# Token-tile square sums issued two units later on TensorE, in the four phases that add to the residual x of a two-layer streaming encoder

## The chip, the cores and the metric

The kernel runs on one core of a Trainium2 chip. The core has five engines with an instruction stream each: TensorE (PE in the rows; its weight loads are PEld), VectorE (DVE), ScalarE (ACT), GpSimd (POOL) and SyncE (SP). The streams meet only at semaphores. Each engine takes its own instructions in order, so an instruction that waits holds up all behind it on that engine. The metric is the device time of one execution in microseconds; the kernel before takes 2903.98 us, the median of three runs (2901.82 to 2904.86).

## The reference

One step over 1024 prompt tokens and 32 sample tokens (1056 in all, 1024 features), two layers, all in float32:

```
for layer in (0, 1):
    x = x + mixer(rmsnorm(x))            # layer 0: RG-LRU + windowed attention, layer 1: mLSTM
    x = x + swiglu(rmsnorm(x))
    x = x + sigmoid(x @ w_gate) * (p[layer] @ w_proj)
y = rmsnorm(x)

rmsnorm(x) = x * rsqrt(mean(x*x over the 1024 features) + 1e-6) * g
```

What matters here is rmsnorm: for every token it needs the sum of squares over all features, so it can't begin for a token before all features of that token's x are done.

## The kernel before, in words

x lies in SBUF with the features on partitions: eight blocks of 128 features (`KT` = 8), each 1056 tokens wide. The tokens are cut into `NT` = 3 tiles of `TW` = 352 columns. Weights come in blocks of 128 output features. SyncE loads a block into one of two `raw` buffers (L400); GpSimd splits it into a high part `wh` (L427) and a low part `wl` (L429), 128x1024 each, in one of four slots, and may take a slot when TensorE has counted it free (`block_done`). A product of float32 precision is three matmuls, high by high, high by low, low by high (`hilo`, L385 to L387). A **unit** is the product of one weight block with one token tile: 8 times 3 = 24 matmuls of 352 columns into one PSUM bank of six.

Four phases add to x: `out0` and `out1` (the output projections of the two mixers) and `gate0` and `gate1` (the last line of each layer). Each is a `tail_phase` of 24 units, numbered 0 to 23 in the order of the table `TAIL` (`out0` starts at unit 8, since its first eight are made earlier). Units 12 to 15 are the last four feature blocks of token tile 0, units 16 to 19 those of tile 1, units 20 to 23 those of tile 2. So after unit 15 token tile 0 is complete, after 19 tile 1, after 23 tile 2. Units 20 to 23 are also the last use of a weight block each; each of them sets a slot free, and GpSimd then splits a block of the next phase into it. TensorE may write unit u when VectorE has emptied the bank of unit u - 6.

For a finished unit the engines do this:

- In the `out` phases VectorE adds the bank to x (L965). In the `gate` phases ScalarE makes the sigmoid of the bank (L1517), VectorE multiplies it with the projection (`prod`, L1033) and adds that to x (L1035).
- ScalarE squares the new x (L1432) into one of two buffers, and VectorE adds the squares into `sqsum` or `sqsum_o` (L895).
- When the squares of all eight feature blocks of a token tile are added, one float32 matmul with a matrix of ones sums them over the partitions (`norm_sum`, L456; the trace has two records for it). It waits for VectorE's add of the tile's last squares: **sum 0** for those of unit 15, **sum 1** for unit 19, **sum 2** for unit 23.
- ScalarE takes the root (`rt`, L1398), VectorE the reciprocal (`rstd`, L857). Then for each of the eight feature blocks VectorE scales x (`tmp`, L906; in `gate1`, where the final norm is made, `ybuf`, L901), ScalarE copies the result to `xh` (L1403), and VectorE subtracts to get `xl` (L914).

VectorE's order around the sums is fixed (`tail_phase` in the vector block). After the add of unit 17 and the squares of 16: reciprocal and half the scaling of tile 0; after unit 18 and the squares of 17: the other half; then unit 19, squares 18, unit 20, squares 19, unit 21, squares 20; then reciprocal and half the scaling of tile 1; unit 22, squares 21; the other half; unit 23, squares 22, squares 23; then the scaling of tile 2. ScalarE's order matches: root 0 stands after the square of unit 17, root 1 after that of unit 21; in the `gate` phases the sigmoid of unit 18 or 22 stands ahead of that square. Sum 2 stands outside `tail_phase`: in `out0` and `out1` inside the first `up` product of the feed-forward, after its units of token tile 0; after `gate0` in the gates' `dense`, after its unit of tile 0; after `gate1` at the end of the program. The first `up` of layer 0 can write its tile 0 only when the bank of unit 23 is empty.

Of the kernel before, what the change touches and what calls it, by code (L numbers as in the profile page):

```python
# [90 lines left out]
def build(nc, I, O):  # L91
    with ExitStack() as ctx:
# [102 lines left out]
        def bank(b, n=TW):  # L195
            return ps[:, b, 0:n]
# [134 lines left out]
        def tail_free(phase, u):  # L331

            return FREE0[phase] + u - SKIP[phase] + 1

        def tail_bank(phase, u):
            return (OFF[phase] + u - SKIP[phase]) % 6
# [16 lines left out]
        def tail_sums(ni):  # L353
            return (sqsum_o, sqb_o) if ni % 2 else (sqsum, sqb_g)

        def sums_at(ni, u):

            return 25 * (ni - 1) + 1 + u + 1
# [24 lines left out]
        def hilo(pe, out, whi, wlo, mhi, mlo, first, last):  # L383

            pe.matmul(out, whi, mhi, start=first, stop=False)  # L385
            pe.matmul(out, whi, mlo, start=False, stop=False)  # L386
            return pe.matmul(out, wlo, mhi, start=False, stop=last)  # L387
# [43 lines left out]
        def split_count(b):  # L431
            return b + 1 + NRAW
# [7 lines left out]
        def _(pe):  # L440
# [11 lines left out]
            def norm_sum(ni, tt):  # L452

                pe.wait_ge(sq_added, sums_at(ni, 12 + 4 * tt + 3))
                pe.wait_ge(rt_ready, 1 + 3 * ni + tt // 2)
                pe.matmul(bank(6 + tt % 2), ones[:, :], tail_sums(ni)[0][:, tt * TW:(tt + 1) * TW],  # L456
                          start=True, stop=True).then_inc(ss_done, 1)

            def tail_phase(phase, b0, ni, xl_at=None):


                for u, (j, tt) in enumerate(TAIL[phase]):
                    if u < SKIP[phase]:
                        continue
                    pe.wait_ge(raw_free, split_count(b0 + j))
                    pe.wait_ge(acc_free, tail_free(phase, u) - 6)
                    slot = (b0 + j) % NW
                    for k in range(KT):
                        if xl_at is not None and j == 0:
                            pe.wait_ge(xl_ready, 1 + xl_at + KT * tt + k + 1)  # L470
                        mm = hilo(pe, bank(tail_bank(phase, u)), wh[:, slot, k, :], wl[:, slot, k, :],
                                  xh[:, k, tt * TW:(tt + 1) * TW], xl[:, k, tt * TW:(tt + 1) * TW],
                                  k == 0, k == KT - 1)
                    mm.then_inc(acc_done if tt < NT - 1 else block_done, 1)
                    if u == 17 or u == 21:
                        norm_sum(ni, (u - 17) // 4)

            def dense(slot, b, free, bank0, xl_at=None, sums=None):

# [207 lines left out]
            def ple(layer, b0):  # L687

                pe.wait_ge(pl_ready, 2 * (layer + 1))
                pe.wait_ge(raw_free, split_count(b0 + 1))  # L690
                for tt in range(NT):
                    for mo in range(KT):
                        u = KT * tt + mo
                        pe.wait_ge(acc_free, FREE0[f"proj{layer}"] - 6 + u + 1)
                        if u < 6:

                            pe.wait_ge(down_added, DA + 24 * FCH * (layer + 1) - 8 + (u + OFF[f"proj{layer}"]) % 6 + 1)
                        slot = (b0 + mo // 4) % NW
                        for kk in range(2):
                            wk = (mo % 4) * 2 + kk  # L700
                            mm = hilo(pe, bank((u + OFF[f"proj{layer}"]) % 6), wh[:, slot, wk, :], wl[:, slot, wk, :],
                                      ph[:, kk, tt * TW:(tt + 1) * TW], pl[:, kk, tt * TW:(tt + 1) * TW],
                                      kk == 0, kk == 1)
                        if u < 23:
                            mm.then_inc(acc_done, 1)
                        else:
                            mm.then_inc(block_done, 2)
                tail_phase(f"gate{layer}", b0 + 2, 2 + 2 * layer, XLN[f"ple{layer}"])
# [16 lines left out]
            attention()  # L725
            pe.wait_ge(mix_low, LOW_O[NQ - 1])
            tail_phase("out0", B0_OUT, 1)
            ffn(0, B0_FFN)
            ple(0, B0_PLE)
# [16 lines left out]
            for half in range(2):  # L746
                for i in range(0, 2):
                    for pr in range(2):
# [4 lines left out]
                        for j in range(CH):  # L753
                            u = CH * pr + j
# [86 lines left out]
            transpose_h(CH - 1)  # L841
            pe.wait_ge(cl_ready, 1 + CH)
            tail_phase("out1", B1_OUT, 3)
            ffn(1, B1_FFN)
            ple(1, B1_PLE)
# [1178 lines left out]
```

## Time and profile before

| | before |
|---|---|
| median of 3 runs | 2903.98 us (2901.82 to 2904.86) |
| profiled execution, its own time | 2904.33 us |
| profiled execution, first to last instruction (span) | 2902.5 us |
| mean granted TensorE clock | 0.977 |
| TensorE matmul busy | 2753.8 us (95%) |
| VectorE busy | 1274.1 us (44%) |
| GpSimd busy | 939.6 us (32%) |
| ScalarE busy | 598.8 us (21%) |

Busy time is read per engine over the whole span. A row of the timeline gives the start in us from the first instruction, the duration in us, the engine, the line of the kernel, operation, output and inputs, the shapes, how many instructions were merged (x2), and in brackets how long the engine had been idle before it and which instruction ended that. The granted clock is a share of 2.4 GHz.

### The profile page before, as it was taken

How to read it: one execution, taken by the hardware profiler on the slowest of the kernel's cores; microseconds unless marked ns; L12 is line 12 of the kernel's file. 1: busy time of each engine (PE TensorE's matmuls, PEld its weight loads, DVE VectorE, ACT ScalarE, POOL GpSimd, SP SyncE). 2: the span in 40 equal slices, each digit the busy share in tenths (PEclk: the TensorE clock that was granted, in tenths of full speed). 3: DMA queues.
4: the chain of work that ended last, by engine and by line, in shares of the span. 5: the costliest groups of instructions: out<-in, count | busy, mean ns of one | idle time of the engine just before them, and what ended most of it. 6: DMA issues, size and time to landing. Idle time of an engine off the chain costs nothing.

```text
span 2902.5 us, 40640 instructions
## 1 busy us (share of the span) xinstructions
PE 2753.8 (95%) x17273; PEld 2686.8 (93%) x17273; DVE 1274.1 (44%) x2070; ACT 598.8 (21%) x1315; POOL 939.6 (32%) x439
## 2 busy tenths in 40 slices
PE   7999998999999999996999998799999999999996
PEld 5898898999999999996999987598999999999996
DVE  7844474333333333557733037537333333333465
ACT  4515322000000000223122145412100000000042
POOL 3222043333334433332434310023433333333430
PEclk9999899999999999998999999999999999999998
DMA  3110121111111111112122221311111111111111
GB/s 135 32 30 30 47 72 38 51 44 44 44 44 44 51 51 45 44 44 105 45 68 84 85 85 54 128 54 44 44 51 44 44 45 51 44 44 44 52 37 60
DMA packets 59765, 160.09 MB, mean 55 GB/s; under 512 B 9276, under 2 KB 30268, under 8 KB 58304
## 3 DMA queue, kind: packets, MB, share of 16 engines
q1 hardware_dynamic: 29952, 109.07, 12.4%
q10 hardware_dynamic: 29632, 48.42, 4.7%
q8 instruction: 137, 2.24, 0.3%
q14 instruction: 44, 0.36, 0.0%
HBM read 137.07 MB, written 20.40 MB: 54 GB/s over the span
## 4 chain that ended last, share of the span: by engine, by line
PE 87%; DVE 7%; ACT 3%; issue 1%; DMA 0%; ACTq 0%; POOL 0%; DVEq 0%; POOLq 0%
PE ps L385 27%; PE ps L387 27%; PE ps L386 27%; DVE tmp L906 1%; PE ps L775 1%; DVE rstd L857 1%; PE ps L587 1%; PE ps L557 1%; PE ps L812 1%; DVE xl L914 1%; DVE hb L1344 1%; PE ps L569 0%; DVE cs L1318 0%; DVE ybuf L901 0%; PE ps L814 0%
## 5 line engine op out<-in xcount | busy, mean ns | idle before, releaser
L385 PE MATMUL ps<-xh,wh 128*128 128x352 f32 x3432 | 1125.3, 328 | 18.0 <-issue 10.3
L386 PE MATMUL ps<-xl,wh 128*128 128x352 f32 x3432 | 1116.3, 325 | 0.0
L387 PE MATMUL ps<-xh,wl 128*128 128x352 f32 x3432 | 1116.0, 325 | 0.0
L427 POOL TENSOR_TENSOR wh<-raw,seeds 128x1024 fp32r<-128x1024 f32 x208 | 419.5, 2017 | 1877.4 <-PE ps L387 1871.9
L385 PEld LDWEIGHTS ps<-xh,wh 128*128 128x128 f32 x3432 | 653.3, 190 | 25.4 <-issue 13.6
L386 PEld LDWEIGHTS ps<-xl,wh 128*128 128x128 f32 x3432 | 653.2, 190 | 2.3 <-issue 1.0
L387 PEld LDWEIGHTS ps<-xh,wl 128*128 128x128 f32 x3432 | 652.8, 190 | 0.0
L429 POOL TENSOR_TENSOR wl<-raw,wh 128x1024 fp32r<-128x1024 f32 x208 | 522.0, 2509 | 16.3
L990 DVE TENSOR_TENSOR tmpb<-ps,tmpa 128x352 f32<-128x352 f32 x132 | 69.0, 524 | 858.5 <-ACT tmpa L1483 857.4
L385 PE MATMUL ps<-hh,wh 128*128 128x352 f32 x1056 | 340.4, 322 | 0.0
L387 PE MATMUL ps<-hh,wl 128*128 128x352 f32 x1056 | 340.0, 322 | 0.0
L386 PE MATMUL ps<-hl,wh 128*128 128x352 f32 x1056 | 340.0, 322 | 0.0
L1005 DVE TENSOR_TENSOR x<-ps,x 128x352 f32<-128x352 f32 x528 | 263.7, 519 | 153.7 <-PE ps L387 153.7
L1483 ACT ACTIVATE tmpa<-ps 128x352 f32<-128x352 f32 x132 | 61.2, 465 | 1283.3 <-PE ps L387 1283.3
L387 PEld LDWEIGHTS ps<-hh,wl 128*128 128x128 f32 x1056 | 198.6, 188 | 0.0
L386 PEld LDWEIGHTS ps<-hl,wh 128*128 128x128 f32 x1056 | 198.5, 188 | 0.0
L385 PEld LDWEIGHTS ps<-hh,wh 128*128 128x128 f32 x1056 | 198.4, 188 | 0.0
L385 PE MATMUL ps<-wh,xh 128*128 128x256 f32 x576 | 163.7, 284 | 0.0
L387 PE MATMUL ps<-wh,xl 128*128 128x256 f32 x576 | 162.1, 281 | 0.0
L386 PE MATMUL ps<-wl,xh 128*128 128x256 f32 x576 | 162.1, 281 | 0.0
L983 DVE TENSOR_TENSOR hl<-tmpb,hh 128x352 fp32r<-128x352 f32 x132 | 159.4, 1221 | 0.3
L386 PEld LDWEIGHTS ps<-wl,xh 128*128 128x128 f32 x576 | 109.7, 190 | 0.0
(252 smaller groups left out, 2354.8 us busy)
## 6 DMA issues: line engine op xcount, KB each, us to landing
raw<-wstream SPq DMA_DIRECT2D x208, 512.0 KB, 3.6
vod<-stage ACTq DMA_DIRECT2D x72, 128.0 KB, 1.9
vb<-vod ACTq DMA_DIRECT2D x9, 512.0 KB, 3.9
ob<-vod ACTq DMA_DIRECT2D x9, 512.0 KB, 3.7
x<-xT ACTq DMA_DIRECT2D x3, 1408.0 KB, 8.5
x<-xT ACTq DMA_DIRECT2D x2, 2112.0 KB, 7.6
xsave<-x ACTq DMA_DIRECT2D x1, 4224.0 KB, 11.4
x<-xsave ACTq DMA_DIRECT2D x1, 4224.0 KB, 14.7
```

Source lines behind the costliest of these rows:

```text
L385: pe.matmul(out, whi, mhi, start=first, stop=False)
L386: pe.matmul(out, whi, mlo, start=False, stop=False)
L387: return pe.matmul(out, wlo, mhi, start=False, stop=last)
L427: pool.tensor_tensor(hi, raw[:, r, :], zero, ALU.add).then_inc(hi_made, 1)
L429: pool.tensor_tensor(lo, raw[:, r, :], hi.bitcast(F32), ALU.subtract).then_inc(raw_free, 1)
L557: mm = pe.matmul(out, qt0[kvh * HD:(kvh + 1) * HD, g, col:col + w], kt[kvh * HD:(kvh + 1) * HD, kcol:kcol + 2 * P], start=True, stop=True)
L587: mm = pe.matmul(ps[0:w, 6, (2 * g + kvh) * HD:(2 * g + kvh + 1) * HD], pts[:, 2 * g + kk, 0:w], vtok[:, vslot + kk, kvh * HD:(kvh + 1) * HD],
L775: mm = pe.matmul(ps[:, b0 + t // 4, (t % 4) * P:(t % 4 + 1) * P], cbd[:, w, t, :], uu[:, t, ds(ucol, P)], start=True, stop=True)
L983: dve.tensor_tensor(hl[:, par, f, tt * TW:(tt + 1) * TW], tmpb[:, v % 2, :], hh[:, par, f, tt * TW:(tt + 1) * TW].bitcast(F32), ALU.subtra ...
L990: dve.tensor_tensor(tmpb[:, v % 2, :], bank(2 * (v % 3) + 1), tmpa[:, v % 2, :], ALU.mult).then_inc(h32_ready, 1)
L1005: dve.tensor_tensor(xs, bank(u % 8), xs, ALU.add).then_inc(down_added, 1)
L1483: act.activation(tmpa[:, v % 2, :], bank(2 * tt), ACT.Silu).then_inc(sil_ready, 1)
```

## The change

In `tail_phase` of the tensor block, sums 0 and 1 stand after units 19 and 23 instead of after units 17 and 21. What they wait for, which squares they sum and their banks stay the same. The streams of the other four engines are the same in both programs.

```
-                    if u == 17 or u == 21:
-                        norm_sum(ni, (u - 17) // 4)
+                    if u == 19 or u == 23:
+                        norm_sum(ni, (u - 19) // 4)
```

TensorE's order in `out0`, before the change, around sum 1 (`sqsum_o` are the added squares, `ones` the matrix of ones, `xh`, `xl`, `wh`, `wl` the high and low parts; the two matmuls ahead are the end of unit 21, those behind it begin unit 22):

```order
L386 MATMUL ps<-xl,wh 128x352
L387 MATMUL ps<-xh,wl 128x352
L456 MATMUL ps<-sqsum_o,ones 128x352 [waits rt_ready,sq_added]
L385 MATMUL ps<-xh,wh 128x352 [waits acc_free,raw_free]
L386 MATMUL ps<-xl,wh 128x352
```

The same sum 1 of `out0` with the change; ahead of it is the end of unit 23, behind it the first `up` product of the feed-forward:

```order
L386 MATMUL ps<-xl,wh 128x352
L387 MATMUL ps<-xh,wl 128x352
L456 MATMUL ps<-sqsum_o,ones 128x352 [waits rt_ready,sq_added]
L385 MATMUL ps<-xh,wh 128x352 [waits xl_ready,acc_free,raw_free]
L386 MATMUL ps<-xl,wh 128x352
```

The sum has moved behind 48 matmuls: no matmul of the phase stands behind it any more.

TensorE's order in `gate0` at the end of unit 17, before the change (sum 0, of `sqsum`):

```order
L386 MATMUL ps<-xl,wh 128x352
L387 MATMUL ps<-xh,wl 128x352
L456 MATMUL ps<-sqsum,ones 128x352 [waits rt_ready,sq_added]
L385 MATMUL ps<-xh,wh 128x352 [waits acc_free,raw_free]
L386 MATMUL ps<-xl,wh 128x352
```

The same place with the change:

```order
L386 MATMUL ps<-xl,wh 128x352
L387 MATMUL ps<-xh,wl 128x352
L385 MATMUL ps<-xh,wh 128x352 [waits acc_free,raw_free]
L386 MATMUL ps<-xl,wh 128x352
L387 MATMUL ps<-xh,wl 128x352
```

Unit 18 follows unit 17 directly; sum 0 now stands 48 matmuls further on, between units 19 and 20.

## Rows read from the trace of the kernel before

**Rows 1.** TensorE's waits: who waited for whom, total us, times, longest.

```profile
PE ps L456 <- DVE sqsum L895: 35.4, 4, 13.0
```

**Rows 2.** Timeline of TensorE in `out0`: sum 0, units 19 and 20, sum 1, `up`.

```profile
409.64 0.75 PE L456 MATMUL ps<-sqsum_o,ones 128*128 128x352 f32 x2
...
414.12 0.32 PE L385 MATMUL ps<-xh,wh 128*128 128x352 f32 x1
...
418.00 0.32 PE L385 MATMUL ps<-xh,wh 128*128 128x352 f32 x1
...
428.37 0.86 PE L456 MATMUL ps<-sqsum_o,ones 128*128 128x352 f32 x2 [2.46 <-DVE sqsum_o L895]
...
448.84 0.63 PE L385 MATMUL ps<-xh,wh 128*128 128x352 f32 x1 [10.33 <-issue]
```

**Rows 3.** Timeline after `out0`: sum 2 and the root that follows it.

```profile
458.81 0.75 PE L456 MATMUL ps<-sqsum_o,ones 128*128 128x352 f32 x2
...
459.61 0.55 ACT L1398 ACTIVATE rt<-ps,vecs 128x352 f32<-128x352 f32 x1 [10.33 <-PE ps L456]
```

**Rows 4.** Timeline of VectorE in `out0`: reciprocal 0, adds of units 18, 19, 23.

```profile
412.80 2.35 DVE L857 RECIPROCAL rstd<-rt 128x352 f32<-128x352 f32 x1 [2.00 <-ACT rt L1398]
...
418.05 0.51 DVE L965 TENSOR_TENSOR x<-ps,x 128x352 f32<-128x352 f32 x1
...
418.92 0.57 DVE L906 SCALAR_TENSOR_TENSOR tmp<-x,vecs,rstd 128x352 f32<-128x352 f32 x1
...
423.51 0.51 DVE L965 TENSOR_TENSOR x<-ps,x 128x352 f32<-128x352 f32 x1
...
448.23 0.51 DVE L965 TENSOR_TENSOR x<-ps,x 128x352 f32<-128x352 f32 x1
```

**Rows 5.** Timeline of GpSimd and VectorE: weight splits beside adds, `out0` then `gate0`.

```profile
422.18 3.16 POOL L427 TENSOR_TENSOR wh<-raw,seeds 128x1024 fp32r<-128x1024 f32 x1 [26.79 <-PE ps L387]
...
1321.16 2.12 POOL L427 TENSOR_TENSOR wh<-raw,seeds 128x1024 fp32r<-128x1024 f32 x1 [31.25 <-PE ps L387]
...
1323.59 2.69 DVE L895 TENSOR_TENSOR sqsum<-sqb_g,sqsum 128x352 f32<-128x352 f32 x1
...
1328.11 2.51 POOL L429 TENSOR_TENSOR wl<-raw,wh 128x1024 fp32r<-128x1024 f32 x1
```

**Rows 6.** Timeline of `gate0`: sums 0, 1 and 2, with VectorE and ScalarE between them.

```profile
1308.34 0.75 PE L456 MATMUL ps<-sqsum,ones 128*128 128x352 f32 x2
...
1315.76 2.35 DVE L857 RECIPROCAL rstd<-rt 128x352 f32<-128x352 f32 x1 [5.21 <-ACT rt L1398]
...
1337.57 1.54 PE L456 MATMUL ps<-sqsum,ones 128*128 128x352 f32 x2 [12.97 <-DVE sqsum L895]
...
1344.33 0.49 ACT L1432 ACTIVATE sqb_g<-x 128x352 f32<-128x352 f32 x1
...
1346.71 2.35 DVE L857 RECIPROCAL rstd<-rt 128x352 f32<-128x352 f32 x1 [7.77 <-ACT rt L1398]
1349.10 4.18 DVE L906 SCALAR_TENSOR_TENSOR tmp<-x,vecs,rstd 128x352 f32<-128x352 f32 x2
...
1363.31 1.54 PE L456 MATMUL ps<-sqsum,ones 128*128 128x352 f32 x2 [11.61 <-DVE sqsum L895]
```

**Rows 7.** Timeline of `out1`: sum 0, reciprocal 1, sum 2.

```profile
1960.65 0.75 PE L456 MATMUL ps<-sqsum_o,ones 128*128 128x352 f32 x2
...
1980.13 2.34 DVE L857 RECIPROCAL rstd<-rt 128x352 f32<-128x352 f32 x1
...
2000.23 1.51 PE L456 MATMUL ps<-sqsum_o,ones 128*128 128x352 f32 x2 [5.73 <-issue]
```

**Rows 8.** Timeline of `gate1`: sum 0 and root 1.

```profile
2852.26 0.75 PE L456 MATMUL ps<-sqsum,ones 128*128 128x352 f32 x2
...
2877.40 0.56 ACT L1398 ACTIVATE rt<-ps,vecs 128x352 f32<-128x352 f32 x1
```

**Rows 9.** Busy us by stretch (PE, PEld, DVE, ACT, POOL), then granted clock and DMA.

```profile
1337.60:1341.10 3.50, 3.50 (x10) 3.00 (x11) 1.31 (x3) 0.01 (x1) 0.00 (x0) 0.51 0.00 0
```

## The prediction

> **What bounds the kernel now.** I began with the table of waits. TensorE is busy 95% of the span, and of its few waits the largest named one is that for VectorE's added squares ahead of the square sums, 35.4 us in four waits [rows 1]. So I read the timeline at the twelve sums. Sum 0 never waits: in `out0` it starts the moment unit 17 ends, at 409.64 [rows 2]. Sum 1 waits 2.46 us there [rows 2] and 12.97 us in `gate0` [rows 6]. Sum 2 waits 11.61 us in `gate0` [rows 6] and 5.73 us in `out1` [rows 7], and in `out0` the first `up` product waits 10.33 us [rows 2] for VectorE's add of unit 23, which starts at 448.23 [rows 4]. Around every tail, then, TensorE's restart hangs on VectorE, and VectorE works through one fixed list from reciprocal 0 to the squares of unit 23. What counts is when that list begins, what slows it, and where it stops to wait for a root. VectorE's share of 44% over the span hides this, since it is full just here.
>
> **What the change removes and adds.** No instruction is added or dropped. A unit takes 3.88 us (414.12 to 418.00) and a sum with the unit behind it 4.48 us (409.64 to 414.12) [rows 2]. Sum 0, which waited for nothing, comes two units, 7.76 us, later. Units 22 and 23 no longer stand behind sum 1, so they run earlier. That removes sum 1's stall from in front of them, but it also ends the weight blocks of units 22 and 23 earlier, and GpSimd splits the next blocks as soon as they end.
>
> **The price of GpSimd beside VectorE.** In `gate0` GpSimd splits two blocks in four instructions from 1321.16 to 1328.11 + 2.51 = 1330.62, 9.46 us [rows 5]. A VectorE add that meets them takes 2.69 us [rows 5] where an add alone follows the next after 0.44 us (418.05 to 418.92 holds two) [rows 4]. In the timeline exactly one such operation gets through for each GpSimd instruction, at its end. So two blocks let four VectorE operations through in 9.46 us, and cost 9.46 - 4 x 0.46 = 7.6 us. With the change units 20 to 23 end 3.88 us apart, which is less than the 4.73 us of a block, so GpSimd works on all four without a pause, 18.9 us, in the middle of VectorE's list: 15.2 us lost. Before, part of this fell on reciprocals and on waits, where it cost nothing.
>
> The Trainium skill ("SBUF — State Buffer", section "Who interferes with whom") says that a VectorE instruction with two SBUF inputs and a GpSimd one share a port pair, and that whichever issues first has it for its whole length. The long add agrees with that. Since by this rule the order of issue decides, VectorE could as well hold GpSimd off; by that alone the sum would lie near the lower of the two bounds that I now take from rows.
>
> The bounds: the first GpSimd instruction of `out0` takes 3.16 us instead of 2.12 [rows 5] and began at 422.18, yet VectorE's add at 423.51 had come after three subtractions of normal length [rows 4]. VectorE can win about three turns at the start: -1.4 us in each phase. The far bound is that VectorE wins always and loses nothing: `out0` would then gain 4.4 us, `out1` 3.7 us, and in `gate0` sum 1 would follow unit 23 directly, which gains 16 us; with `gate1` below -25 us in all. The other end is that each pair of blocks costs 1 us more, as the 3.16 us instruction does: +2 us in each of three phases. I take 15.2 us, since every turn after the first alternates.
>
> **`out0`.** Sum 0 at 409.64 + 7.76 = 417.40, the root 0.80 us after the sum's start and 0.55 us long [rows 3], reciprocal 0 at 418.8, where it was 412.80 [rows 4]: +6.0. VectorE's clean list from there: 10.71 us to the add of unit 19 (412.80 to 423.51) [rows 4], then four operations of 0.44, 12.5 us to the squares of unit 19. Unit 20 ends at 422.0, as before (sum 0 moves from in front of unit 18 to in front of unit 20), so GpSimd's four blocks run from 422.2 to 441.1, and all 15.2 us fall into the list. Sum 1 at 418.8 + 12.5 + 15.2 = 446.5. TensorE, done with unit 23 at 433.6, waits 13 us for it instead of 2.46. The root follows the sum's start by 0.8 us, or by 1.6 us if the sum runs at the lower clock, where it takes 1.54 us instead of 0.75 [rows 3, 6]; I take 1.2, then 0.6 for the root itself. Reciprocal 1 at 448.3. From here nothing of GpSimd is left: 10.71 us to the add of unit 23, and 0.61 us from its start to TensorE's first `up` matmul (448.23 to 448.84) [rows 2, 4]. `up` starts at 459.6, +10.8 us. What follows it keeps its distances.
>
> **`out1`** has the same geometry. Sum 0 at 1968.41 [rows 7], reciprocal 0 at 1969.8, sum 1 27.7 us later at 1997.5, reciprocal 1 at 1999.3 where it was 1980.13 [rows 7]. TensorE's tile-0 `up` units no longer bridge the time to sum 1; they start behind it and end before 2008. Sum 2 needs the squares of unit 23: 10.71 us to the add of unit 23 and 1.7 us for that add, the two squares and ScalarE's square between them. Sum 2 at 2011.7 instead of 2000.23 [rows 7]: +11.5 us.
>
> **`gate0`** had the largest stall, and gains least from its going. Reciprocal 0 came at 1315.76 because ScalarE made the sigmoid of unit 18 first [rows 6]; now sum 0 is last, at 1316.10, and the reciprocal comes at 1317.5, +1.7. From there to sum 1 it was 21.8 us with two blocks split on the way [rows 6]; two more blocks add 7.6 us. Sum 1 at 1346.9. Here the root is also behind the square of unit 21: VectorE needs 1.0 us more for that x, and from ScalarE's square to the reciprocal it is 2.38 us (1344.33 to 1346.71) [rows 6], the load of the root's function table among it. Reciprocal 1 at 1350.3, +3.6. Behind it two scalings no longer meet GpSimd, 1.08 us instead of 4.18 [rows 6]: -3.1. Sum 2, and all behind it: +0.5 us. VectorE's idle time of 7.77 us ahead of reciprocal 1 [rows 6] shrinks to about 2, and the collisions eat what that frees.
>
> **`gate1`** has no weights left to split. Sum 0 at 2860.02, four units behind it, sum 1 at 2860.02 + 4.48 + 3 x 3.88 = 2876.14, with its squares added some 4 us earlier. Root 1 at 2876.9 instead of 2877.40 [rows 8]: -0.5 us, and the end follows.
>
> **Sum.** 10.8 + 11.5 + 0.5 - 0.5 = +22.3 us on the profiled execution's own 2904.33 us: 2926.6. That execution lies 0.35 us above the median of the runs, so the forecast is 2926.3 us.
>
> **TensorE's clock.** After the 12.97 us stall it ran at 0.51 of 2.4 GHz, that is at the 1.2 GHz level, for 3.5 us [rows 6, 9], which costs 1.7 us where TensorE is what bounds. `out0` and `out1` have this restart before as well as after. If the longer idle time doubles the slow stretch at both, the sum grows by 3.4 us, to 2929.7; if `out1` restarts at full clock, it shrinks by 1. The Trainium skill ("TensorE: Matmul & The Clock Gate", section "HAM oscillation — how this bites in real kernels") has it that idle gaps bring the slow clock and the work behind them pays; the trace agrees.
>
> **Rivals.**
>
> 1. *TensorE is the bound, and the stalls at sum 1 simply go.* For it: 95% busy, and 2.46 + 12.97 us of stall stand in front of work that needs no sum. This gives -15.4 us, and -1.7 us for the slow stretch behind the long one: 2887. Against it: the stall comes back at the next thing that needs VectorE, as after sum 1 in `out0`, where `up` waited 10.33 us anyway [rows 2]. It would need a VectorE list with slack, and the rows show none. With it goes the far bound above (VectorE wins every turn, 2879). Chance 0.04.
> 2. *The delay is absorbed.* TensorE's list ends each phase with waits of 5 to 12 us; if sum 0 had slack of 7.76 us nothing would change, 2904. Against it: reciprocal 0 in `out0` stood 3.2 us behind sum 0's start [rows 2, 4], which leaves 1.8 us of slack, not 7.8. Chance 0.03.
> 3. *Only the start is late, the collisions do not grow.* If VectorE loses to GpSimd what it lost before (in `out0` 35.4 us from reciprocal 0 to the add of unit 23 [rows 4], less 24.1 us of clean work: 11.3), then `out0` pays 6.0 and 0.9 for the root's wait, `out1` 7.4 and 0.9, `gate0` gains 4.1, `gate1` 0.5: +10.6 us, 2914.6. For it: GpSimd's total work is the same. Against it: four blocks now fall together into pure VectorE work. Chance 0.12.
> 4. *The forecast*, with -4 to +6 us from the collisions and -1 to +3.4 from the clock: 2919 to 2932. Chance 0.78. Above that, by both adding up, 0.03.
>
> **Range and chances.** About 0.2%, 6 us, is what a measurement of this kernel can tell from no change. Faster by more: rival 1, 0.04. Within: 0.03. Slower by more: 0.93. The range runs from rival 3's value to the upper end of the forecast, 2914 to 2932.
>
> **What would show it.** In the changed kernel's timeline: sum 0 at 417.4 and reciprocal 0 at 418.8; GpSimd's eight instructions in `out0` without a pause from 422.2 to 441, with eight VectorE operations of over 1.5 us beside them; sum 1 waiting about 13 us in each of the first three phases and not at all in `gate1`; `up` in `out0` starting near 459.6; distance from sum 0 to sum 2 in `gate0` shorter by 7 us than before. I am wrong if sum 1 comes before 440 in `out0`, or if GpSimd pauses between blocks, or if what follows the late restart is shorter than before.

## The result, and the profile after

| | before | with the change |
|---|---|---|
| first comparison, median (lowest to highest) | 2904.42 us (2901.82 to 2908.62) | 2925.43 us (2919.58 to 2928.55) |
| ratio, 95% interval | | 1.0069 (1.0048 to 1.0089) |
| second comparison, other runs | 2905.13 us | 2923.82 us, ratio 1.0072 (1.006 to 1.0085) |
| profiled execution, span | 2902.5 us | 2917.7 us |
| TensorE matmul busy | 2753.8 us | 2747.2 us |

The change makes the kernel slower by 0.7%: 21.0 us in the first comparison, 18.7 us in the second; 2926.3 us was forecast. TensorE is busy for no longer than before. What grew are its waits. In the table of TensorE's waits after the change (who waited for whom, total us, times, longest), the sums now wait in three phases for about 12.6 to 14.6 us each:

```profile
PE ps L456 <- DVE sqsum L895: 35.9, 3, 14.6
PE ps L456 <- DVE sqsum_o L895: 25.1, 2, 12.6
...
PE ps L385 <- issue: 12.0, 1, 12.0
```

The row on `sqsum` reads like that of before [rows 1], since `gate0` and `gate1` changed little. The row on `sqsum_o` is new in size: 12.56 us ahead of sum 1 in each of `out0` and `out1`, where it had been 2.46 in `out0` [rows 2].

The timeline of `out0` after the change, TensorE, ScalarE, VectorE and GpSimd; it answers to [rows 2, 4, 5]:

```profile
412.24 0.75 PE L456 MATMUL ps<-sqsum_o,ones 128*128 128x352 f32 x2
413.03 0.55 ACT L1398 ACTIVATE rt<-ps,vecs 128x352 f32<-128x352 f32 x1 [5.99 <-PE ps L456]
413.61 2.35 DVE L857 RECIPROCAL rstd<-rt 128x352 f32<-128x352 f32 x1 [7.97 <-ACT rt L1398]
417.02 2.31 POOL L427 TENSOR_TENSOR wh<-raw,seeds 128x1024 fp32r<-128x1024 f32 x1 [26.80 <-PE ps L387]
...
426.70 2.17 POOL L427 TENSOR_TENSOR wh<-raw,seeds 128x1024 fp32r<-128x1024 f32 x1
...
433.67 2.50 POOL L429 TENSOR_TENSOR wl<-raw,wh 128x1024 fp32r<-128x1024 f32 x1
441.07 1.54 PE L456 MATMUL ps<-sqsum_o,ones 128*128 128x352 f32 x2 [12.56 <-DVE sqsum_o L895]
443.24 2.35 DVE L857 RECIPROCAL rstd<-rt 128x352 f32<-128x352 f32 x1 [1.35 <-ACT rt L1398]
454.57 0.63 PE L385 MATMUL ps<-xh,wh 128*128 128x352 f32 x1 [11.95 <-issue]
```

Sum 0 starts at 412.24, so unit 17 ended 7.76 us earlier, at 404.48. This execution had come there 5.2 us sooner than that of before (409.64), through instructions that the change doesn't touch. So I compare distances, from the end of unit 17 to the point where TensorE goes on for good. The other rows say how VectorE got there. The root waited for sum 0, VectorE for the root (7.97 us idle). GpSimd's eight instructions run from 417.02 to 433.67 + 2.50 = 436.17 without a pause, 19.15 us; the third block starts at 426.70, 22.2 us behind unit 17. Before, GpSimd had paused there until the late unit 22 ended, and the third block started 25.1 us behind unit 17. That row of the kernel before:

```profile
434.78 2.66 POOL L427 TENSOR_TENSOR wh<-raw,seeds 128x1024 fp32r<-128x1024 f32 x1 [2.11 <-PE ps L387]
```

VectorE in the same stretch of the changed kernel, one operation for each GpSimd instruction, all of over 2.2 us save the one that reads a PSUM bank (L965):

```profile
417.49 2.22 DVE L914 TENSOR_TENSOR xl<-tmp,xh 128x352 fp32r<-128x352 f32 x1
419.64 2.71 DVE L906 SCALAR_TENSOR_TENSOR tmp<-x,vecs,rstd 128x352 f32<-128x352 f32 x1
422.27 2.21 DVE L914 TENSOR_TENSOR xl<-tmp,xh 128x352 fp32r<-128x352 f32 x1
424.40 0.51 DVE L965 TENSOR_TENSOR x<-ps,x 128x352 f32<-128x352 f32 x1
424.83 2.28 DVE L895 TENSOR_TENSOR sqsum_o<-sqb_o,sqsum_o 128x352 f32<-128x352 f32 x1
427.04 2.21 DVE L906 SCALAR_TENSOR_TENSOR tmp<-x,vecs,rstd 128x352 f32<-128x352 f32 x1
429.18 2.66 DVE L914 TENSOR_TENSOR xl<-tmp,xh 128x352 fp32r<-128x352 f32 x1
431.76 2.21 DVE L906 SCALAR_TENSOR_TENSOR tmp<-x,vecs,rstd 128x352 f32<-128x352 f32 x1
433.89 2.66 DVE L914 TENSOR_TENSOR xl<-tmp,xh 128x352 fp32r<-128x352 f32 x1
```

The sums of the other phases after the change, which answer to [rows 6 to 8] (`gate0`, `out1`, `gate1`):

```profile
1320.98 0.75 PE L456 MATMUL ps<-sqsum,ones 128*128 128x352 f32 x2
1351.89 1.54 PE L456 MATMUL ps<-sqsum,ones 128*128 128x352 f32 x2 [14.64 <-DVE sqsum L895]
...
1368.75 1.54 PE L456 MATMUL ps<-sqsum,ones 128*128 128x352 f32 x2 [10.60 <-DVE sqsum L895]
...
1973.33 0.75 PE L456 MATMUL ps<-sqsum_o,ones 128*128 128x352 f32 x2
2002.16 1.54 PE L456 MATMUL ps<-sqsum_o,ones 128*128 128x352 f32 x2 [12.56 <-DVE sqsum_o L895]
...
2016.74 0.93 PE L456 MATMUL ps<-sqsum_o,ones 128*128 128x352 f32 x2 [3.70 <-issue]
...
2875.65 0.75 PE L456 MATMUL ps<-sqsum,ones 128*128 128x352 f32 x2
2891.75 0.75 PE L456 MATMUL ps<-sqsum,ones 128*128 128x352 f32 x2
...
2903.14 1.54 PE L456 MATMUL ps<-sqsum,ones 128*128 128x352 f32 x2 [10.64 <-DVE sqsum L895]
```

From these and the rows of before, the distance from the end of unit 17 (7.76 us ahead of sum 0 where that is late) to `up` in `out0` and to sum 2 in the other phases:

| kernel | out0 | gate0 | out1 | gate1 | sum of differences |
|---|---|---|---|---|---|
| before | 39.20 | 54.97 | 39.58 | 35.74 | |
| changed | 50.09 | 55.53 | 51.17 | 35.25 | +22.55 |
| changed, second profile | 50.09 | 55.53 | 51.19 | 35.25 | +22.57 |
| forecast difference | +10.8 | +0.5 | +11.5 | -0.5 | +22.3 |
| measured difference | +10.89 | +0.56 | +11.59 | -0.49 | |

In the span, 15.2 us of difference appear: +22.55, less the 5.2 us ahead of the first moved instruction, less 2.2 us between the phases, of which 0.84 us lie in the restart of `out0` (from `up` to sum 2 it is 9.13 us instead of 9.97) and 0.88 us behind sum 2 of `out1`. From the end of unit 17 in `out0` to the end of the program the changed kernel took 20.4 us longer, in its second profile 21.9 us. The medians moved by 21.0 and 18.7 us.

### The profile page after: what moved, and what is told of

It is laid out like the page before. It is cut to its first block, busy times and chain, and to the rows that moved or that the text cites. A ratio compares the mean times of both kernels' runs of the same rounds, so it can differ in the third digit from the quotient of the medians.

```text
span 2917.7 us, 40640 instructions
## 1 busy us (share of the span) xinstructions
PE 2747.2 (94%) x17273; PEld 2679.5 (92%) x17273; DVE 1285.2 (44%) x2070; ACT 598.7 (21%) x1315; POOL 941.0 (32%) x439
## 4 chain that ended last, share of the span: by engine, by line
PE 87%; DVE 8%; ACT 3%; issue 1%; DMA 0%; ACTq 0%; DVEq 0%
PE ps L385 27%; PE ps L387 27%; PE ps L386 27%; DVE tmp L906 1%; DVE xl L914 1%; PE ps L775 1%; DVE rstd L857 1%; PE ps L557 1%; PE ps L812 1%; PE ps L587 1%; DVE hb L1344 1%; PE ps L569 0%; DVE cs L1318 0%; PE ps L814 0%; PE ps L456 0%
## 5 line engine op out<-in xcount | busy, mean ns | idle before, releaser
L385 PEld LDWEIGHTS ps<-xh,wh 128*128 128x128 f32 x3432 | 651.2, 190 | 28.2 <-issue 16.2
## 6 DMA issues: line engine op xcount, KB each, us to landing
x<-xsave ACTq DMA_DIRECT2D x1, 4224.0 KB, 14.6
```

## The experiments

Every kernel was timed beside the kernel before; distances are from its profile. An edit can shift the line numbers by one or two.

**Only sum 0 late** (sum 1 stays behind unit 21):

```
-                    if u == 17 or u == 21:
-                        norm_sum(ni, (u - 17) // 4)
+                    if u == 19 or u == 21:
+                        norm_sum(ni, (u - 19) // 2)
```

> Only sum 0 moves (behind unit 19), sum 1 stays behind unit 21. Theory (late start of VectorE's list plus its collisions with GpSimd): +10.8 us in out0 (end of unit 17 to first up matmul 50.0 us instead of 39.2), +11.7 in out1 (end of unit 17 to sum 2: 51.3 instead of 39.6), +1.7 in gate0, +1.7 in gate1, +25.9 us in all, about 2930 us: more than the full change. Rival (what costs is that units 22 and 23 run early and four weight blocks are split together): most of the loss is gone, below +8 us in all.

Measured: 2932.21 us, ratio 1.0094 (1.008 to 1.0108), slower than the full change. The distances are 49.61 us in `out0` (+10.4), 51.25 in `out1` (+11.7), 57.85 in `gate0` (+2.9) and 38.99 in `gate1` (+3.2), +28.2 in all. The rival falls. The sums of this kernel, `out0` then `gate1`:

```profile
417.04 0.75 PE L456 MATMUL ps<-sqsum_o,ones 128*128 128x352 f32 x2
...
438.22 1.54 PE L456 MATMUL ps<-sqsum_o,ones 128*128 128x352 f32 x2 [12.67 <-DVE sqsum_o L895]
...
458.89 0.63 PE L385 MATMUL ps<-xh,wh 128*128 128x352 f32 x1 [10.68 <-issue]
...
2897.30 0.86 PE L456 MATMUL ps<-sqsum,ones 128*128 128x352 f32 x2 [3.66 <-DVE sqsum L895]
```

In `out0` the path is another one, sum 1 7.7 us sooner than in the changed kernel and two blocks split behind it, but `up` comes at almost the same distance: the same list of VectorE, the same four blocks against it. The two gates missed their expectation by 1.2 and 1.5 us. There ScalarE makes root 1 only after the sigmoid of unit 22, and unit 22 stands behind a stall at sum 1 (14.79 us in `gate0`, 3.66 in `gate1`). It ran longer at the 1.2 GHz level than before: in `gate0` the granted clock was 0.50 from 1350 to 1356, some 6 us, where it had been 0.51 for 3.5 us [rows 9]; in `gate1` it was 0.50 from 2899 to 2901, where before it had stayed at 1.00 (2870.4 to 2874.4). From sum 1 to reciprocal 1 it took 10.2 us in `gate0` and 9.05 us in `gate1`, where before it took 9.14 and 7.52.

**Only sum 1 late**:

```
+                    if u == 17 or u == 23:
+                        norm_sum(ni, (u - 17) // 6)
```

> Only sum 1 moves (behind unit 23), sum 0 stays behind unit 17. Theory: +0.5 us in out0, +1.2 in out1, -1.2 in gate0, -0.5 in gate1, 0.0 in all, about 2904 us; sum 1 doesn't wait in out0, out1 and gate1, and waits about 13 us in gate0, where GpSimd splits four blocks without a pause. Rival (early units 22 and 23 and the four splits together are the cause): most of the +21 us is here.

Measured: 2904.37 us, ratio 0.9998 (0.9989 to 1.0007), no change. Distances 40.05 in `out0` (+0.85), 53.76 in `gate0` (-1.2), 40.00 in `out1` (+0.4, where +1.2 was expected), 35.25 in `gate1` (-0.5). Sum 1 and `up` in `out0`, sum 1 in `gate0`:

```profile
432.61 0.75 PE L456 MATMUL ps<-sqsum_o,ones 128*128 128x352 f32 x2
...
448.80 0.63 PE L385 MATMUL ps<-xh,wh 128*128 128x352 f32 x1 [15.44 <-issue]
...
1345.52 1.54 PE L456 MATMUL ps<-sqsum,ones 128*128 128x352 f32 x2 [12.87 <-DVE sqsum L895]
```

In `out0` the stall of 2.46 us is gone from sum 1, and the wait of `up` has grown from 10.33 to 15.44 us. In `gate0` the stall of 12.97 us became one of 12.87 us behind unit 23: the freed units ran early, GpSimd split four blocks without a pause (1321.46 to 1340.42), and VectorE had eight long operations in front of sum 1 instead of four. So the loss belongs to sum 0, and moving sum 1 alone neither costs nor gives.

**The changed kernel again.**

> The changed kernel itself, beside the others. Theory: +21 to +22.5 us over the kernel before, 2926 us, and again +10.9, +11.6, +0.6 and -0.5 us from the end of unit 17 in out0, out1, gate0, gate1. Rival (part of the +21 us is spread between executions): the four distances differ from the first profile by more than 1 us.

Measured: 2923.82 us, ratio 1.0072 (1.006 to 1.0085). That is +18.7 us, where +21 to +22.5 were expected. The distances are those of the table above, equal to the first profile within 0.02 us. So the spread between the two executions lies outside the tails: this one reached the end of unit 17 in `out0` 2.5 us ahead of the kernel before, the first one 5.2 us.

**Only the gates changed**:

```
+                    first = 19 if ni % 2 == 0 else 17
+                    if u == first or u == first + 4:
+                        norm_sum(ni, (u - first) // 4)
```

> Both sums move, but only in gate0 and gate1; out0 and out1 are as before. Theory: +0.5 us in gate0, -0.5 in gate1, no change in all, about 2904 us, although the stall of 13 us at sum 1 in gate0 is still there, now 14.6 us long and behind unit 23. Rival (the stall's going should pay, the out phases spoil it): -10 us or more.

Measured: 2904.79 us, ratio 1.0 (0.9992 to 1.0009); `gate0` +0.56, `gate1` -0.49, stall at sum 1 14.64 us. The loss is all in `out0` and `out1`.

**Short splits, before and changed.** In the 12 blocks split beside the tails GpSimd works on 8 columns of 1024 and leaves the other 1016 unsplit:

```
+                    b = NW * i + j
+                    n = 8 if any(s <= b < s + NW for s in (B0_FFN, B1_GATE, B1_FFN)) else KT * P
...
+                    pool.tensor_tensor(hi, raw[:, r, 0:n], zero[:, 0:n], ALU.add).then_inc(hi_made, 1)
```

> The kernel before, with GpSimd splitting only 8 of 1024 columns in the four weight blocks that follow each tail (12 blocks in all; the products made with them are left wrong). Theory (VectorE's list is what the restarts wait for, and collisions with GpSimd lengthen it): end of unit 17 to up in out0 29.0 us instead of 39.2, to sum 2 in out1 32.5 instead of 39.6, to sum 2 in gate0 42.6 instead of 55.0: about 2875 us. Rival (collisions don't reach TensorE's restarts): distances as before, 2904 us.

> The changed kernel with the same short splits. Theory: out0 36.7 us, out1 37.8, gate0 40.3, gate1 35.2: +7.7, +5.3, -2.3, -0.5 against the kernel before with short splits, so that only +10 us of the +21 is left, about 2885 us; the rest of the loss is the collisions of four blocks split together. Rival (the loss is all from the late start, collisions only move): +21 us remains.

| | time, ratio to before | out0 | gate0 | out1 | gate1 |
|---|---|---|---|---|---|
| before, short splits | 2875.02 us, 0.9891 (0.9876 to 0.9906) | 29.17 | 44.19 | 32.21 | 35.67 |
| changed, short splits | 2882.36 us, 0.9924 (0.9911 to 0.9936) | 36.58 | 40.29 | 37.67 | 35.25 |
| difference | +7.3 us | +7.4 | -3.9 | +5.5 | -0.4 |

Six of the seven distances that were forecast came within 0.3 us; `gate0` of before missed by 1.6 us. I put this down to its unit 22, again at the 1.2 GHz level behind a stall of 5.43 us (granted clock 0.50 from 1319.5 to 1321.5), which held up root 1: reciprocal 1 came 8.99 us behind sum 1. The collisions cost the kernel before 30 us, 28.3 of them in the four distances. Without them the change adds 8.6 us to the distances instead of 22.6, 7.3 us to the time (about 10 were expected), and in `gate0` it gains. In `out1` 5.5 us are left of a start that is 7.4 us later, since in the kernel before with short splits sum 2 waited for nothing there and had slack. The changed kernel with short splits, GpSimd's first split, VectorE beside it, sum 1 and `up`:

```profile
419.78 0.62 POOL L429 TENSOR_TENSOR wh<-raw,seeds 128x8 fp32r<-128x8 f32 x1 [26.80 <-PE ps L387]
...
420.26 0.52 DVE L916 TENSOR_TENSOR xl<-tmp,xh 128x352 fp32r<-128x352 f32 x1
...
431.11 0.75 PE L458 MATMUL ps<-sqsum_o,ones 128*128 128x352 f32 x2
...
443.82 0.63 PE L385 MATMUL ps<-xh,wh 128*128 128x352 f32 x1 [11.96 <-issue]
```

VectorE's operations keep their 0.52 us, sum 1 waits for nothing, and `up` still waits 11.96 us for VectorE: that part is the late start alone.

**Half of tile 1's scaling behind unit 23.** The sums stand as before; VectorE (and ScalarE in the same way) does work that nobody waits for yet behind work that TensorE does wait for:

```
-                    if u == 18 or u == 22:
-                        scaled_part(ni, (u - 18) // 4, 4, KT)
+                    if u == 18:
+                        scaled_part(ni, 0, 4, KT)
                 add_squares(ni, 23)
+                scaled_part(ni, 1, 4, KT)
```

> Sums as in the kernel before. VectorE and ScalarE do the second half of the scaling of token tile 1 behind the squares of unit 23 instead of between units 22 and 23. If VectorE's list is what TensorE waits for, the work that sum 2 and the first up product don't need can stand behind it: up in out0 starts 10 us earlier (reciprocal 2 9 us earlier), sum 2 in out1 4.6 us and its tile-2 products 2.9 us earlier, gate0 -2.2, gate1 -2.0, in all -16 us, about 2888 us. Rival (TensorE's clock and GpSimd set the end of the phases): no gain above 4 us.

Measured: 2891.68 us, ratio 0.9953 (0.9941 to 0.9966): 13 us faster than the kernel before, where 16 were expected. `up` in `out0` came at 32.72 us (-6.5, not -10), sum 2 in `out1` at 34.99 (-4.6, as expected), in `gate0` at 52.06 (-2.9), but there reciprocal 2 came no sooner than before (57.72 us instead of 57.13 behind unit 17), since ScalarE's second half now stood in front of its root. In `gate1` sum 2 came at 35.29 (-0.45), and the program ended 52.18 us behind unit 17 instead of 50.24, 1.9 us later, where 2 us sooner had been expected.

So the gates gave nothing, and the profile shows less than the median does. From the end of unit 17 in `out0` to the end of the program this execution is 7.6 us shorter than that of before; another 4.4 us lie ahead of that point, in instructions that the edit doesn't touch. How much of the 13 us is the order's stays open. What was missed in `out0` is in VectorE's rows of this kernel:

```profile
430.42 2.22 DVE L906 SCALAR_TENSOR_TENSOR tmp<-x,vecs,rstd 128x352 f32<-128x352 f32 x1
432.56 2.70 DVE L914 TENSOR_TENSOR xl<-tmp,xh 128x352 fp32r<-128x352 f32 x1
435.19 0.51 DVE L966 TENSOR_TENSOR x<-ps,x 128x352 f32<-128x352 f32 x1
435.62 1.77 DVE L895 TENSOR_TENSOR sqsum_o<-sqb_o,sqsum_o 128x352 f32<-128x352 f32 x1
437.32 0.51 DVE L966 TENSOR_TENSOR x<-ps,x 128x352 f32<-128x352 f32 x1
437.75 2.88 DVE L895 TENSOR_TENSOR sqsum_o<-sqb_o,sqsum_o 128x352 f32<-128x352 f32 x2
```

The add of unit 23 (437.32) had moved up into GpSimd's splits, with three long operations in front of it behind reciprocal 1.

**Combined**: that order in the `out` phases, and in the gates only sum 1 behind unit 23.

> out0 and out1 with the second half of the scaling of tile 1 behind the squares of unit 23, sums as before; gate0 and gate1 with VectorE and ScalarE as before and only sum 1 moved behind unit 23. From the distances of half_behind in the out phases (-6.5 and -2.3 us) and of sum1_late in the gates (-1.2 and -0.5, where half_behind had gained nothing on reciprocal 2): 3 to 4 us below half_behind, about 2888 us. Rival (half_behind's gain came from the gates): no better than 2900.

Measured: 2890.08 us, ratio 0.9951 (0.9939 to 0.9964). It is 15 us below the kernel before, and 1.6 us below the last one, which the intervals don't tell apart; 3 to 4 us below it were expected. From unit 17 of `out0` to the end its profile is 8.7 us shorter than that of before. The gates did as expected (53.76 and 35.25). `out0` came at 34.99 us instead of the 32.72 that the same code had shown: in this execution unit 22 ran at full clock (granted 1.00 from 428.7 on, against 0.51 and 0.64 in the first and second 2 us behind sum 1 of the last kernel), units 22 and 23 ended sooner, and GpSimd began the last two blocks at 433.53, 4.81 us behind sum 1 (428.72) instead of 6.44. VectorE then met all four of their instructions before its add of unit 22, not two:

```profile
433.53 1.91 POOL L427 TENSOR_TENSOR wh<-raw,seeds 128x1024 fp32r<-128x1024 f32 x1 [0.47 <-PE ps L387]
...
440.27 2.50 POOL L429 TENSOR_TENSOR wl<-raw,wh 128x1024 fp32r<-128x1024 f32 x1
...
443.51 0.51 DVE L967 TENSOR_TENSOR x<-ps,x 128x352 f32<-128x352 f32 x1
```

These are two executions, one of each kernel; that the clock made the difference is read from their rows and not tested by itself.

## Why the prediction was right

- *VectorE's list sets TensorE's restart.* Shown: with sum 0 late TensorE's waits grow and its busy time doesn't, and moving half a scaling out of the list brings `up` in `out0` 6.5 us and sum 2 in `out1` 4.6 us forward.
- *Late start, +6.0 us in `out0`, +7.4 in `out1`.* Reciprocal 0 came 9.13 us behind unit 17 in both (413.61 - 404.48 in `out0`), forecast 9.2. With short splits the difference in `out0` is 7.4 us, of which 6.0 is this, the rest the wait of root 1 for sum 1 behind unit 23.
- *Collisions, 15.2 us for four blocks.* GpSimd took 19.15 us for eight instructions instead of the 18.9 assumed, with eight long VectorE operations beside them. Sum 1 came 28.83 us behind sum 0 in both `out` phases, forecast 29.1. The three turns that VectorE had won at the start of the first split before [rows 4, 5] did not come here: its first operation beside GpSimd took 2.22 us. Of the +22.6 us in the distances 14 vanish when the splits are short.
- *`gate0`, +0.5 us.* The stall at sum 1 grew from 12.97 to 14.64 us and VectorE's idle time ahead of reciprocal 1 fell from 7.77 to 1.99 us, both as worked out.
- *`gate1`, -0.5 us*: sum 1 without a wait, root 1 on its heels.
- *Rival 1* (the stalls simply go) fell with sum 1 alone: three stalls gone and the fourth moved, and no time gained. *Rival 2* (the delay is absorbed) fell with the result, whose interval starts at 1.0048. *Rival 3* (collisions don't grow, +10.6 us) fell with the distances, +22.55 us, and with the short splits: the 14 us that vanish there are collisions that the kernel before did not have.
- *TensorE's clock.* The upper term, +3.4 us for slow stretches of double length at both restarts, did not come. In the first profile the restarts of `out0` and `out1` gave back 0.84 and 0.88 us, the latter where sum 2 took 0.93 us instead of 1.51 (forecast: 1 us less if `out1` restarts at full clock). In the second profile they cost 0.6 and 0.3 us more than before. Where the clock did count, in the gates with only sum 0 late, it was through ScalarE's wait for unit 22, which I hadn't priced. That is argued from the rows and the slow stretches beside them; no run took the clock away.
- *Luck.* The four distances came within about 0.1 us of the forecast each, which is the mechanism. That the first median lies 0.9 us from 2926.3 is closer than the method allows: the second lies 2.5 us from it, and executions of one kernel differ by several us in stretches that the change doesn't touch.
- *Slips.* The terms of the far bound add up to 24.6 us, not to over 25. The terms of rival 4 (-4 to +6 and -1 to +3.4 around 2926.3) give 2921 to 2936, not 2919 to 2932. Neither touches the sum of +22.3 us.

The full change costs less than sum 0 alone (22.6 against 28.2 us in the distances, 18.7 against 27.1 us in times taken side by side), since in the gates the late sum 1 gives back what the late sum 0 takes.

## What to carry to other kernels

A stall that a profile shows in front of an instruction can be worth nothing by itself, as the 12.97 us here: find the list of work on the other engine that ends it, and ask whether the edit shortens that list, starts it sooner or slows it. An instruction that waits for nothing and opens another engine's work (sum 0) must not be delayed by more than that work has slack (1.8 us in `out0` here, against a delay of 7.76), even if nothing on its own engine minds. Work that starts early because a stall is gone can collide with the critical engine; price it by how many of that engine's operations get through per foreign instruction.

## What the runs showed of the hardware

While GpSimd runs a 128x1024 float32 add or subtraction back to back, VectorE completes one operation with two SBUF inputs for each, 2.2 to 2.7 us instead of 0.52, be it an add, a subtraction or a scaling (1.8 to 2.3 us behind an operation that reads PSUM); those that read a PSUM bank keep 0.51 us, and the reciprocal with its one input keeps 2.35. An exception stands at the start of a stream: in `out0` of the kernel before three subtractions kept their length, and GpSimd's first instruction took 3.16 us. The collisions cost 30 us in 12 of 208 blocks. A phase in which TensorE's unit 22 ran faster was longer, as GpSimd started earlier inside VectorE's list (34.99 against 32.72 us, two executions).
